# Input projections of a first block as three rounded products, their parts kept in places that a recurrence holds later

## The reference, cut to what matters

```
h    = modulate(x, norm_mix_w[0], shift, scale)     # latent and context tokens
proj = h @ ev_w_in[0]                               # 1024 -> 3584
# columns: q, f of direction 0, f of direction 1, values, gate of the recurrence;
#          u and v of the token mixer
y    = even_mixer(...)  @ ev_w_out[0]
x    = x + g1 * y ;  then a convolutional FFN, the second layer, the second block
```

## Time and profile before

| | |
|---|---|
| median of 3 runs | 2702.7 us |
| profiled execution, its own time | 2700.53 us |
| its span in the trace | 2698.7 us |
| PE busy | 2514.8 us (93%) |
| DVE, ACT, POOL busy | 931.2, 854.4, 718.8 us |
| `features`, L736: 640 records | 215.0 us busy |
| `w_low` on POOL, L446 | 556.9 us busy in 239 |
| `w_high` on ACT, L439 | 245.8 us busy in 239 |

### The profile page before, as it was taken

How to read it: one execution, slowest core, us unless ns; L and a number is a source line. 1 busy time by engine, 2 the same in 40 slices (tenths; PEclk the granted TensorE clock), 3 DMA queues, 4 the chain that set the end, 5 groups by cost and what they waited for, 6 DMA issues and landing times.

```text
span 2698.7 us, 34861 instructions
## 1 busy us (share of the span) xinstructions
PE 2514.8 (93%) x13605; PEld 1991.1 (74%) x13605; DVE 931.2 (35%) x1597; ACT 854.4 (32%) x1298; POOL 718.8 (27%) x435
## 2 busy tenths in 40 slices
PE   6999999959899999998999998999998999889997
PEld 3676666658788888887888567888787886677766
DVE  3662654042422223333123223322344003731173
ACT  3222223122322222233321233433343225633362
POOL 0240231002222222233231002444344442024302
PEclk9999999979899999998887999999998999989998
DMA  7166058101121121121210001233222231112211
GB/s 308 44 259 263 32 193 318 55 31 55 47 62 62 62 62 55 62 63 47 84 47 24 1 1 63 79 100 93 86 93 98 95 101 66 49 55 78 77 46 63
DMA packets 54926, 234.78 MB, mean 87 GB/s; under 512 B 6112, under 2 KB 7392, under 8 KB 52256
## 3 DMA queue, kind: packets, MB, share of 16 engines
q1 hardware_dynamic: 54576, 232.44, 25.1%
q0 software_dynamic: 240, 0.79, 0.1%
HBM read 231.11 MB, written 2.10 MB: 86 GB/s over the span
## 4 chain that ended last, share of the span: by engine, by line
PE 84%; issue 5%; DVE 5%; ACT 3%; DMA 3%; POOL 1%; SPq 0%; DVEq 0%; ACTq 0%; POOLq 0%
PE ps L763 14%; PE ps L764 14%; PE ps L765 14%; PE ps L736 7%; PE ps L1321 4%; PE ps L1323 4%; PE ps L1324 4%; PE ps L583 2%; DMA XB<-ada_dram 2%; PE ps L1144 2%; PE ps L746 2%; PE ps L1416 1%; PE ps L1217 1%; PE ps L1414 1%; PE ps L1510 1%
## 5 line engine op out<-in xcount | busy, mean ns | idle before, releaser
L446 POOL TENSOR_TENSOR w_low<-ring,w_high 128x1024 fp32r<-128x1024 f32 (+2 forms) x239 | 556.9, 2331 | 1471.1 <-ACT w_high L439 1471.1
L439 ACT ACTIVATE w_high<-ring 128x1024 fp32r<-128x1024 f32 (+2 forms) x239 | 245.8, 1031 | 990.9 <-PE ps L765 683.0
L763 PE MATMUL ps<-h_high,w_high 128*128 128x512 f32 x1104 | 437.2, 396 | 12.3 <-DVE h_low L684 11.6
L764 PE MATMUL ps<-h_low,w_high 128*128 128x512 f32 x1104 | 434.8, 394 | 0.0
L765 PE MATMUL ps<-h_high,w_low 128*128 128x512 f32 x1104 | 434.1, 393 | 0.0
L763 PEld LDWEIGHTS ps<-h_high,w_high 128*128 128x128 f32 x1104 | 210.6, 191 | 58.6 <-issue 12.3
L765 PEld LDWEIGHTS ps<-h_high,w_low 128*128 128x128 f32 x1104 | 210.1, 190 | 44.9
L764 PEld LDWEIGHTS ps<-h_low,w_high 128*128 128x128 f32 x1104 | 210.7, 191 | 41.8
L736 PE MATMUL ps<-Hbuf,ring 128*128 128x512 f32 (+1 forms) x640 | 215.0, 497 | 3.7 <-ACT Hbuf L669 2.2
L1321 PE MATMUL ps<-hidden,w_high 128*128 128x512 f32 (+1 forms) x528 | 190.3, 360 | 14.6 <-issue 14.6
L736 PEld LDWEIGHTS ps<-Hbuf,ring 128*128 128x128 f32 x640 | 123.5, 194 | 96.0 <-issue 86.3
(11 more groups left out here) (262 smaller groups left out, 4183.8 us busy)
## 6 DMA issues: line engine op xcount, KB each, us to landing
XB<-ada_dram SPq DMA_DIRECT2D x84, 768.0 KB, 6.6
ring<-up_dram SPq DMA_DIRECT2D x88, 512.0 KB, 3.5
ring<-down_dram SPq DMA_DIRECT2D x44, 512.0 KB, 3.5
ring<-winE_dram SPq DMA_DIRECT2D x32, 512.0 KB, 3.5
ring<-win_dram SPq DMA_DIRECT2D x10, 1024.0 KB, 5.6
ring<-winC_dram SPq DMA_DIRECT2D x20, 512.0 KB, 3.4
arena<-ada_dram SPq DMA_DIRECT2D x12, 768.0 KB, 20.8
XB<-xl_dram SPq DMA_DIRECT2D x2, 2048.0 KB, 9.3
```

Source lines behind the costliest of these rows:

```text
L439: nc.scalar.activation(WH[p][:, 0:L], RAW[p][:, 0:L], ACT.Copy).then_inc(w_hi, 1)
L446: nc.gpsimd.tensor_tensor(WL[p][:, 0:L], RAW[p][:, 0:L], WH[p][:, 0:L].bitcast(F32), ALU.subtract)\
L763: nc.tensor.matmul(bank[:, 0:n], wh[:, cols], hi, start=(k == 0), stop=False)
L764: nc.tensor.matmul(bank[:, 0:n], wh[:, cols], lo, start=False, stop=False)
```

## The change

`win0`, `win1` and `wmlp` move to the split form: 10, 10 and 8 chunks of 512 KB. Chunks 6 and 7 of `win0` and `win1`, and 4 to 7 of `wmlp`, are value chunks; each of them holds half of the 1024 rows for 256 columns, and pairs of token tiles now share one bank of sums. `features`, `tokens`, `load_chunk` and `release` are gone.

The input's parts would need 16 tiles of S columns and do not fit beside the recurrence. `in_part` lays them out: the first four in the buffer of squares, three in rows 2 and 3 of `Y` (in the last round in `WK[0]`), one in the buffer of the added squares, and the others in `WK[1]`, `ACC`, `KD`, `ST` and `QB`. They are written three times. For `win0` norm n0 writes them (`shift_high`, `scale_parted`, `odd_lows`). For `win1` and `wmlp` ACT and POOL write them again from the whole `h` in `Hbuf` while the recurrence runs out (`part_high`, `part_low`): tiles 0 to 3 after step 4's scores, 4 to 7 after step 5's, the context after the last outputs. ACT shifts the even tiles of `Hbuf` later (`shift_even`).

The core of the diff:

```diff
 SPLIT = dict(
-    wout0=(8, D), up0=(2 * FT, D), ...
+    win0=(10, D), win1=(10, D), wmlp=(8, D), wout0=(8, D), up0=(2 * FT, D), ...
...
@@ PE
             def win_chunk(r, c):
-                w = await_chunk(pe, win, c)
...
+                if c in (6, 7):
+                    split_values(pe, win, c, in_tok_parts(r))
                 else:
+                    split_features(pe, win, c, win, 2 * c if c < 6 else 2 * c - 1, KT, P, in_parts(r), (0, 1),
+                                   ready=None if c else in_there(pe, r) if r else h_there(pe, "n0"))
...
-                if r == 0:
-                    win_chunk(1, 0)
-                else:
-                    mlp_chunk(0)
+                for c in range(2):
+                    if r == 0:
+                        win_chunk(1, c)
+                    else:
+                        mlp_chunk(c)
@@ ACT
             mod_row(4)
+            for k in range(2):
+                split_hi("win0", k)
             mod_row(5)
             for k in range(2):
-                shift_whole("n0", k)
+                shift_high("n0", k)
...
+                    if not (r and c < 2):
+                        split_hi(win, c + 2)
+                if r == 0:
+                    for s in range(2):
+                        shift_even("n0", s)
...
+                for d in range(2):
+                    act.wait_ge(hg_f, 2 * r + d + 1)
+                    A(A_b[d][:, :, :], A_b[d][:, :, :], ACT.Ln).then_inc(hg_ln, 1)
+                split_hi(win, 8)
...
-                for n in range(2):
-                    for x in range(2):
-                        exps(n, x)
+                for x in range(2):
+                    exps(0, x)
+                split_hi(win, 9)
...
+                    if n == 4:
+                        for k in range(2):
+                            split_hi(following, k)
+                        act.wait_ge(h_ready, KT)
+                        await_sums(act, SS, (NL + 1) * 4 + NL)
+                        part_high(r + 1, 0, range(4))
+                    if n == 5:
+                        await_sums(act, SS, (NL + 1) * 5 + NL)
+                        part_high(r + 1, 0, range(4, KT))
+                await_sums(act, SU, 11)
+                part_high(r + 1, 1)
@@ POOL
+                if n == 1:
+                    await_sums(pool, f"win{r}", 18)
...
             for r in range(2):
-                for n in range(6):
+                for c in range(4 if r else 2, 8):
+                    split_lo(win, c)
+                differences(r, 0, (win, 8))
+                split_lo(win, 9)
+                for n in range(1, 6):
                     differences(r, n)
+                for c in range(2):
+                    split_lo(following, c)
+                part_low(r + 1)
@@ DVE
                 for n in range(6):
-                    if n < 5:
+                    if 0 < n < 5:
                         operands(n + 1)
                     mask_scores(n)
+                    if n == 0:
+                        operands(1)
@@ SP
-            for k in range(3):
-                load_chunk(sp, "win0", k, k)
+            for k in range(2):
+                load_split(sp, "win0", k, k)
             for k in range(2):
                 await_taken(sp, *spread_sum("n0", k))
             load_mods(range(ADA_SLOTS))
-            for k in range(3, 5):
-                load_chunk(sp, "win0", k, k)
+            for k in range(2, 10):
+                load_split(sp, "win0", k, k)
@@ ACT, ahead of sv and wout0
+                if c == 0:
+                    split_hi("wmlp", 7)
+                    split_hi("wout0", 0)
             act.wait_ge(mlp_u, 1)
...
+            split_hi("wout0", 1)
...
-            for k in range(2):
-                split_hi("wout0", k)
```

More of the change, by code:

```diff
@@ L85 @@
 SPLIT = dict(
-    wout0=(8, D), up0=(2 * FT, D), down0=(FT, D), winM=(8, D), qb=(9, 3 * P), kvb=(6, 4 * P), woutM=(8, D),
+    win0=(10, D), win1=(10, D), wmlp=(8, D), wout0=(8, D), up0=(2 * FT, D), down0=(FT, D), winM=(8, D), qb=(9, 3 * P), kvb=(6, 4 * P), woutM=(8, D),
     up1=(2 * FT, D), down1=(FT, D), winE=(32, D), woutE=(8, D), winC=(20, D), woutC=(8, D),
@@ L219, in two_blocks @@
         small = sb("small", 96)
+        with nc.sbuf_tensor("squares_rounded", [P, NSQ, S], F32R) as place:
+            SQR = place[:]
         SQ = sb("SQ", NSQ, S)
@@ L356, in await_all_taken @@
                 await_taken(eng, stage, k)
[L358 to L370, removed]
-            eng.dma_start(ring[:, s, 0:L], dram[stage][row]).then_inc(slot_full[s], 16)
         def split_use(stage, k, pairs=0):
@@ L717, in modulated @@
                               [mod[:, l, 24 * which + k, s:s + 1] for k in range(KT)],
-                              hi and [hi[:, k, :] for k in range(KT)], lo and [lo[:, k, :] for k in range(KT)]))
+                              highs, lows))
             return items
@@ L788, in split_values @@
             wh, wl = await_parts(pe, stage, c)
-            (first, n, per, width), place, last, _ = v_chunk(stage, c)
+            (_, _, per, width, first_sum, tiles_), place, last, _ = v_chunk(stage, c)
             share = 512 // width
-            for t in range(4):
-                k_sum = first + t // share
+            for t in range(tiles_):
+                k_sum = first_sum + t // share
                 if place == 0 and t % share == 0:
@@ L1091, in _ @@
             for stage, (n, _) in SPLIT.items():
-                first = 2 if SPLIT_BEFORE[stage] == 0 else 0
-                for k in range(first):
-                    load_split(sp, stage, k, k)
-                if stage in ("woutE", "woutC"):
-                    first = 2
+                if stage in ("win0", "win1", "wmlp"):
+                    continue
+                first = 2 if stage in ("woutE", "woutC") else 0
                 with sp.Fori(first // 2, n // 2) as i:
@@ L1270, in _ @@
             hgrn(1)
-            for c in range(1, 4):
+            for c in range(2, 8):
                 mlp_chunk(c)
@@ L1956, in _ @@
                 pool.dma_start(to, dram[name]).then_inc(mlp_tab, 16)
+            for c in range(4, 8):
+                split_lo("wmlp", c)
             parted = dict(up0="n1", winM="n2", up1="n3", winE="n4", winC="n5")
             for stage, (n, _) in SPLIT.items():
+                if stage in ("win0", "win1", "wmlp"):
+                    continue
                 first = 0
@@ L2555, in laid_out @@
     narrow = [r(c * P, (c + 1) * P) for c in range(64)]
-    even = [r(c * 256, (c + 1) * 256) for c in range(64)]
     def col(v):
@@ L2581, in in_runs @@
     def in_runs(chunks, w, runs):
-        for first, n, per, width in runs:
-            v = w[:, P * first:P * first + width].reshape(n, per, P, width)
-            chunks[first:first + n] = v.transpose(0, 2, 1, 3).reshape(n, P, -1)
+        for first, n, per, width, _, _ in runs:
+            chunks[first:first + n] = value_chunks(w, P * first, n, per, width)
         return chunks
```

241 lines of the change are left out of this document (129 added, 112 removed).

## The result

The changed kernel takes 2682.8 us (median of 5), the kernel before 2705.8 (median of 5): ratio 0.992, 95% interval 0.9902 to 0.9938, so 23 us less. The forecast was 56.2 less, and the measured time is outside the range (2631 to 2668).

A forecast was written before the change was run, and what follows sets the result against it. PE, busy 93% of the span, was taken as the bound. Savings of 9.1 (win0), 10.6, 16.0, 12.2 and 8.3 us sum to 56.2 off the 2702.7 median: 2646 us, own range 2638 to 2656, wider range 2631 to 2668.

The forecast's parts named there:

- step f: Recurrence: step 1's differences wait for win0's last sum, operands ready after some 14.3 us, PE there after 14.1; costed at nothing.
- rival 3: Recurrence loses its lead: PE waits 7.7 us for POOL's differences in each of 12 steps, 2738 us, slower; chance 0.04.
- a, one tile: win0 on PE: 8.34 us a tile in split form, two value chunks 17.3; 84.0 us in all, 23.4 less.
- b, end of first chunk: Start of win0: later modulation row and scaling, then norm n1's pace; first chunk ends at 58.0, 6.7 us lost.
- c, before third chunk: win0's third chunk: its weights stand behind four modulation loads in SP's list; 4.1 us lost.
- d, clock in `win0`: win0: PE runs partly at the lower clock after the longer stops; 2 us lost.
- e, the two late chunks: win0, chunks 8 and 9: weights parted behind the gate chain come 1.1 and 0.4 us late; 1.5 lost.
- g, first chunk of `win1`, `wmlp`: First chunk of win1 and of wmlp: 22.0 to 16.7 us, 5.3 less, twice, 10.6 in all.
- j, way to `wout0`: Start of wout0: weights parted before the mixer's products, PE then waits for y's first rest; 8.3 us less.
- Rival 1: PE's stops in win0 are hidden, weights landing early and the clock staying up: 2632 to 2638 us; chance 0.16.
- Rival 2: Parting of weights shows: POOL, slowed beside DVE, exceeds the chunk's cover; about 2663 us; chance 0.20.
- Rival 4: Projection products from scattered places miss wout0's pitch, halfway between the two forms: 31 us less, 2677; chance 0.06.

The follow-up runs named there:

- run 4: Changed kernel with step 1's differences, exps and operands back ahead of the recurrence, some products reading other tiles' parts (wrong operands, same work): 2653.1 us.
- Run 5: Changed kernel with POOL's differences of steps 2 and 3 waiting until DVE is through the operands of the step before: 2675.3 us.
- run 1: The changed kernel again, unedited: 2680.9 us, the kernel before 2706.1.
- run 3: Changed kernel with the weights of win0's chunks 2 and 3 loaded before the pieces of modulation weights: 2671.1 us.
- runs 2: Changed kernel with DVE making masks of scores 1 and results of step 0 before operands of step 2: 2682.1 us.
- 11: Changed kernel with POOL's earlier step 1 start, followers' old places, win0's chunks 2 and 3 loaded early, and DVE's masks and results before operands of step 2: 2661.7 us.
- kernel 8: Changed kernel with step 1's exps and operands in their old list places, POOL still waiting for the projection's last sum: 2684.0 us.
- kernels 9: Changed kernel with ACT making the last modulation row before win0's first two rounded weights: 2675.6 us.
- 12: Kernel 11 plus the last modulation row made before the two rounded weights at the start: 2665.2 us.

## Why the prediction was wrong

The sign, the path and most terms were right; **step f** failed, "So it just fits, and I cost it at nothing". The recurrences are 31.3 us longer in the profiled execution (19.1 and 12.2), of which 4 lie at the end of round 0 and not in the lost lead; run 4 puts the lead at 27.8 by medians. What was right and wrong in it, piece by piece:

- POOL's 7.7 us were right (146.01 to 153.75).
- "ACT and DVE then 6 to 7 more" was 11.3: step 1's last operand was ready at 165.07, 19.3 us after the recurrence's start and not 14.3. The estimate divided busy times by six, and so took DVE's operands at the rate that they have while POOL rests. Run 5 shows 5.27 us where they took 10.5 beside POOL.
- "PE comes to step 1 after 14.1 us and takes these operands last": it came after 12.9 (158.65), and its first score already needs the first eight.
- What is queued behind the late operands was not followed. The masks of step 1 and `results` of step 0 stand behind the operands of step 2 on DVE, and `updates` of step 1 wait for them: 6.25 us, the longest stop. The step asked only when step 1 is ready.
- "without the cover each us late is a us" was too little: PE's work in these stretches also ran at a lower clock, 9.5 and 5.6 us more busy time, with a granted clock of 0.88 and 0.91 for 0.97.
- "The lead comes back" was right: from the third pass on they take 14 to 16 us. That is why rival 3, which named this very mechanism, was wrong in size: it priced 12 steps at 7.7 us each, 92 us, where one pass in each round lost 12 (26.2 for 14.3) and the one ahead of it 1 to 2 more. It also had a chance of 0.04. A rival with the same cause and one bad pass a round would have come near the result.

The other terms, forecast and profiled:

| step | forecast | measured |
|---|---|---|
| a, one tile | 8.34 | 8.4 (second tile, 61.33 to 69.7) |
| b, end of first chunk | 58.0, 6.7 lost | 61.3, 10.0 lost |
| c, before third chunk | 4.1 | 5.50 (POOL, as said) |
| d, clock in `win0` | 2.0 | 1.4 behind the third chunk's stop; 2.6 more within b |
| e, the two late chunks | 1.5 | 0.43 + 0.47 |
| g, first chunk of `win1`, `wmlp` | 16.7 | 18.3 both |
| h, rest of `win1` | 70.3 | 71.3 |
| i, rest of `wmlp` | 52.8 | 52.4 |
| j, way to `wout0` | 8.3 less | 5.9 less |

Step b lost three more: the loads were there at 40.0 and 41.3, not 38.3 and 39.7, and DVE's small gain operation took 1.87 us beside POOL's first `w_low`; the row of the modulation came at 42.23, the scaling at 45.87 instead of 42.7. Step d: products at 0.43 us apart instead of 0.23 ran for some 13 products after the first stop (2.6 us) and 7 after the second (1.4); the 2.6 lie within step b's 10.0 and are not to be added. Step j: PE's start before the mixer's products came 2.3 us later behind `wmlp`; the wait at `wout0` is 5.35 us for y's rest, as forecast, and not for `w_low`. `win0` ended at 145.8 for 141.3, 4.5 us short, and g to j are 6.2 short. With the recurrences' 31.3 that is 42.0 off the forecast 56.2, which leaves 14.2; the two profiled executions differ by 13.6. By medians, on run 1's chip, the change gave 25.2 us, so 31.0 are missing, and run 4 gives back 27.8 of them: the lost lead is nine tenths of the shortfall. The third chunk's stop was priced (4.1 and a part of d's 2.0), so only its excess of 1.4 us belongs there.

Rival 1 (stops hidden) did not come; run 3 shows that one of them could have been. Rival 2 (parting shows) did not either: PE waited for `w_low` at the three places named and nowhere else in `win0`. Rival 4 is out by the pitch. The test of the prediction was right: "wrong if the recurrence's stretch is longer than 101 us".

## What to carry to other kernels

When operands are put into space that a later stage writes, ask when that stage's first writer used to start, and follow the late start through every helper's list, two steps far, not to the first consumer alone. Release such a place by the part that is in the way, and read that part first: 5.5 us of earlier release were worth some 19 us here with the followers moved along, 8 without (not clear of noise), and moving the followers alone nothing. Here stops of the busiest engine also cost clock (1.6 us behind one of 5.5), so price them above their length; and a reordering inside one late queue only moved the stop (runs 2 and 11).

## What the hardware showed that was not expected

- **DVE and POOL slow each other, on ordinary multiplications, and not always in the same way.** Eight DVE products of 128x256 with both inputs in the arena take 2.77 us while POOL rests and 6.33 beside its subtractions; four of 128x512 2.50 and 4.17. POOL's own go from 0.61 to 0.79 us. The masks, whose data come from `ps`, stay at 0.75 to 0.76 each beside POOL. The Trainium skill ("GPSIMD Engine Reference", table at its head) says that POOL shares its memory interfaces with DVE instructions that have two inputs in SBUF or run in a two-port mode; these rows agree. The prediction cited that rule for the scans and did not apply it to the operands. But who pays changes. In kernel 8 POOL's first subtraction of step 3 starts 1.83 us behind DVE's operands of step 2 in both rounds. In round 0 (the first two rows) it is held 3.82 us while DVE keeps its full rate; in round 1 both run on, and DVE is slow:

```profile
170.21 2.76 DVE L2144 TENSOR_TENSOR arena<-arena 128x256 f32<-128x256 f32 x8
172.04 3.82 POOL L1956 TENSOR_TENSOR arena<-arena 128x256 f32<-128x256 f32 x1 [7.83 <-PE ps L1205]
...
385.89 3.61 DVE L2144 TENSOR_TENSOR arena<-arena 128x256 f32<-128x256 f32 x8
387.72 0.74 POOL L1956 TENSOR_TENSOR arena<-arena 128x256 f32<-128x256 f32 x1 [7.82 <-PE ps L1205]
```

  What decides it is not shown.
- **The clock is low behind a short stop, with a long stream already waiting.** In `win0` the stop of 5.50 us was followed by seven products 0.43 us apart, 3 us in all, ahead of the others at 0.23; without the stop (run 3) the stretch had a granted clock of 0.98 for 0.93.
- **The same stop recurs almost to a hundredth:** 6.18 to 6.26 us, in both rounds, on different chips, at step 1 or 2. It is no fixed cost of the chip but the same list worked off at the same rates from the same release. Where POOL was the one held, so that the operands took 2.77 + 2.50 us instead of 3.61 + 4.20, it was 3.50 to 3.67: in both rounds of kernels 9 and 11, and in one round each of 8 and 12. So a recurrence can be some 2.6 us shorter or longer by this alone, which is as much as several of the orders compared above differ by.
